# Causal mixers that project x before its root is known, with the root multiplied in behind the product

## The reference

```python
def first_block(x, norm_mix, w_in, w_pool, pool_scale, attn_gain, w_out, norm_ffn, ...):
    for l in range(DEPTH):
        h = rmsnorm(x, norm_mix[l])
        x = x + hybrid_mixer(h, w_in[l], w_pool[l], pool_scale[l], attn_gain[l], w_out[l])
        h = rmsnorm(x, norm_ffn[l])
        ...

def hybrid_mixer(h, w_in, w_pool, pool_scale, attn_gain, w_out):
    proj = h @ w_in
    u = proj[..., :D_POOL]
    q, k, v = jnp.split(proj[..., D_POOL:], 3, axis=-1)
    y_a = pool_mixer(u, w_pool, pool_scale)
    o = dilated_attention(to_heads(q), to_heads(k), to_heads(v))
    y_b = rmsnorm(o..., attn_gain)
    return jnp.concatenate([y_a, y_b], axis=-1) @ w_out
```

## Time and profile before

| | us |
|---|---|
| median of 3 runs | 2465.37 (2464.77 to 2465.46) |
| the profiled execution, its own time | 2464.63 |
| its span, from the first to the last instruction | 2462.4 |
| TensorE busy | 2427.3 (99%) |
| DVE busy | 2077.8 (84%) |
| ACT busy | 1576.1 (64%) |
| GpSimd busy | 172.1 (7%) |

### The profile page before, as it was taken

The page is one execution under the profiler, slowest core; times in us unless marked ns, Lnnn a source line. Parts: engine busy times, 40 slices in busy tenths (PEclk is TensorE's granted clock), DMA queues, the critical chain, the costliest instruction groups (busy, mean ns, idle before and its releaser), DMA issues.

```text
span 2462.4 us, 44463 instructions
## 1 busy us (share of the span) xinstructions
PE 2427.3 (99%) x17074; PEld 2223.3 (90%) x17074; DVE 2077.8 (84%) x2848; ACT 1576.1 (64%) x2312; POOL 172.1 (7%) x244
## 2 busy tenths in 40 slices
PE   9999999999999999999999999999999999999999
PEld 9999998999999999899998899988899899988998
DVE  5788867999999999999999799786898898787665
ACT  5644565888888888888887544557544544567543
POOL 2111021000000000000000111011011011010000
PEclk9999999999999999999999999999999999999999
DMA  7698554999999999999999688443688587432542
GB/s 297 230 364 312 201 180 174 395 361 378 364 384 365 381 371 396 396 396 398 396 385 376 220 320 308 162 146 129 240 314 304 215 319 291 155 129 81 219 181 76
DMA packets 136640, 696.22 MB, mean 283 GB/s; under 512 B 16528, under 2 KB 16656, under 8 KB 87728
## 3 DMA queue, kind: packets, MB, share of 16 engines
q1 hardware_dynamic: 109872, 598.79, 64.6%
q0 software_dynamic: 23424, 88.16, 9.4%
q10 hardware_dynamic: 3136, 6.43, 0.7%
HBM read 683.29 MB, written 13.24 MB: 283 GB/s over the span
## 4 chain that ended last, share of the span: by engine, by line
PE 86%; DVE 8%; ACT 4%; issue 2%; POOL 0%; DVEq 0%; ACTq 0%; POOLq 0%
PE ps L2451 16%; PE ps L2047 15%; PE ps L2048 15%; PE ps L2049 15%; PE ps L2617 10%; PE ps L2453 8%; DVE w_parts L1733 2%; DVE a_parts L1741 1%; ACT w_parts L1140 1%; DVE w_parts L1354 1%; PE ps L2072 1%; PE ps L2583 1%; PE ps L2076 1%; ACT w_parts L824 1%; DVE xT L1376 0%
## 5 line engine op out<-in xcount | busy, mean ns | idle before, releaser
L2451 PE MATMUL ps<-a_parts,w_parts 128*128 128x512 f32 x1760 | 618.8, 394 | 1.4 <-DVE a_parts L1319 1.0
L1733 DVE TENSOR_TENSOR w_parts<-ring,w_parts 128x1024 fp32r<-128x1024 f32 x448 | 548.3, 1224 | 42.3 <-ACT w_parts L1140 36.8
L2047 PE MATMUL ps<-w_parts 128*112 128x256 f32 x1792 | 517.0, 289 | 0.0
L2048 PE MATMUL ps<-w_parts 128*112 128x256 f32 x1792 | 500.1, 279 | 0.0
L2049 PE MATMUL ps<-w_parts 128*112 128x256 f32 x1792 | 500.0, 279 | 0.0
L2453 PE MATMUL ps<-a_parts,w_parts 128*128 128x256 f32 x1760 | 493.5, 280 | 0.0
L1140 ACT ACTIVATE w_parts<-ring 128x1024 fp32r<-128x1024 f32 x448 | 471.7, 1053 | 0.0
L2451 PEld LDWEIGHTS ps<-a_parts,w_parts 128*128 128x128 f32 x1760 | 329.9, 187 | 74.7 <-issue 3.5
L2453 PEld LDWEIGHTS ps<-a_parts,w_parts 128*128 128x128 f32 x1760 | 333.0, 189 | 0.0
L2048 PEld LDWEIGHTS ps<-w_parts 128*112 128x112 f32 x1792 | 313.3, 175 | 11.6
L2047 PEld LDWEIGHTS ps<-w_parts 128*112 128x112 f32 x1792 | 313.6, 175 | 10.9 <-issue 0.2
(11 more groups left out here) (286 smaller groups left out, 4379.2 us busy)
## 6 DMA issues: line engine op xcount, KB each, us to landing
ring<-wstream SPq DMA_DIRECT2D x378, 1024.0 KB, 7.3
ring<-wstream SPq DMA_DIRECT2D x378, 512.0 KB, 5.9
proj<-astream POOLq DMA_DIRECT2D x144, 512.0 KB, 5.8
slot_rows<-branch POOLq DMA_DIRECT2D x7, 448.0 KB, 7.3
slot_out<-slot_rows POOLq DMA_DIRECT2D x1, 3136.0 KB, 15.1
sq<-slot_rows ACTq DMA_DIRECT2D x49, 64.0 KB, 5.4
slot_out<-pT ACTq DMA_DIRECT2D x49, 64.0 KB, 5.4
vtok<-crow POOLq DMA_DIRECT2D x3, 512.0 KB, 4.3
```

The costliest lines, as they stand in the source:

```text
L1733: nc.vector.tensor_tensor(up_lo[:, n % 2, at], ring[:, s, at], up_hi[:, n % 2, at], ALU.subtract)\
L2047: mm(o, stationary[0], moving[0], start=start, stop=False, skip_group_check=True)
L2048: mm(o, stationary[0], moving[1], start=False, stop=False, skip_group_check=True)
L2451: mm(ps[:, bank, :], hi, a_parts[:, :, k, :], start=k == 0, stop=k == KB - 1, skip_group_check=True)
```

## The change

- In norms 0 and 2 (`RAW`) `hT` is no longer made. ACT writes `a_hi` as x times norm weight, beside each square; DVE makes the rest of the same product by one scalar_tensor_tensor with x and `a_hi` (`raw_rest`). In norm 2 these rests stand between the residual adds, two blocks behind.
- The head of tile 0 in norm 0 is split in thirds of 1024 between these, where it was in halves.
- TensorE starts the product first and makes the five sums just before block 7 of tile 0. The six fillers of these two norms are gone, and `WARM` goes from 24 to 30.
- ACT makes the root behind tile 1's high parts, into a row of its own (`root_row`).
- The units that are not values are copied by DVE (`scaled_unit`), which multiplies the root row and the constant scale in. They take their places among DVE's other work in the mixer, and the rests of tiles 2 to 4 are queued as halves between them. Units 0 to 3 go to banks 4, 5, 7 and 0.
- For the values the root is wanted by token: TensorE turns the root row by two fp32 matmuls of one column each into bank 7, ACT copies it, and ACT's copies of units 12 to 15 take it as their scale and wait for the twelve scaled units.

The diff, cut:

```diff
-WARM = 24
+WARM = 30
...
             if m < 2:
-                return n if n < 4 else 4 + n % 2
+                return (4, 5, 7, 0)[n] if n < 4 else 4 + n % 2
...
# ACT, norm(n)
                 for k in range(KB):
...
+                    if n in RAW:
+                        nc.scalar.activation(a_hi[:, k, :], xT[:, k, :], ACT.Identity,
+                                             scale=V("norm_mix", (n // 2) * KB + k)).then_inc(ah_ready, 1)
+                        if n == 0 and k in (1, 3, 5):
+                            head(0, k // 2)
                     nc.scalar.activation(sq[:, k, :], xT[:, k, :], ACT.Square,
...
-                if n == 0:
-                    head(n, 0)
+                if n in RAW:
+                    opened()
+                    hi_tile(HEADS[n], 1)
                 act.wait_ge(ss_ready, norm_at(n) + 1)
-                inverse_root(norm_s[:, 1, :], norm_s[:, 0, :], SS[:, 0:T],
+                inverse_root(root_row[:, :] if n in RAW else norm_s[:, 1, :], norm_s[:, 0, :], SS[:, 0:T],
...
# ACT, in_copies: values
+                            act.wait_ge(in_copied, UNITS_BEFORE[m] + IN1_F * FB)
+                            act.wait_ge(by_token, m + 1)
+                            nc.scalar.activation(vtok[:, tt, a:b], ps[:, bank, 0:b - a], ACT.Identity,
+                                                 scale=root_of[:, tt:tt + 1]).then_inc(in_copied, 1)
...
# ACT, mixer1
                 in_copies(m, 6, 8)
+                act.wait_ge(token_roots, m + 1)
+                nc.scalar.activation(root_of[:, :], ps[:, 7, 0:TT], ACT.Copy).then_inc(by_token, 1)
                 copy_turned(u)
...
# DVE
+                if n == 0:
+                    for k in range(KB):
+                        raw_rest(n, k)
+                        if k in (1, 3, 5):
+                            head(0, k // 2)
+                elif n == 2:
+                    head(2, 1)
...
+            def raw_rest(n, k):
+                dve.wait_ge(ah_ready, KB * SPLIT_INPUTS.index(f"n{n}") + k + 1)
+                if n:
+                    dve.wait_ge(x_ready, KB * (n - 1) + k + 1)
+                nc.vector.scalar_tensor_tensor(a_lo[:, k, :], xT[:, k, :], V("norm_mix", (n // 2) * KB + k),
+                                               a_hi[:, k, :], ALU.mult, ALU.subtract).then_inc(as_ready, 1)
...
# DVE, residual(r, gate=None, early=None, raw=None)
                 for k in range(KB):
+                    if raw and k >= 2:
+                        raw_rest(raw, k - 2)
...
+                for k in (KB - 2, KB - 1) if raw else ():
+                    raw_rest(raw, k)
...
# DVE, mixer1
-                lo_tiles(stage, [2])
+                def lo_part(i, h):
+                    lo(stage, i, *tile_half(stage, i, h), 2 * (SPLITS[stage] + i) + h, h == 1)
+
+                def scaled_unit(n):
+                    wait_unit(dve, m, n)
+                    if 4 <= n < 8:
+                        dst, scale = upad[:, n - 4, 16:16 + T], 1.0
+                    else:
+                        dst, scale = proj[:, QKV_DST[n], :], HD ** -0.5 if n in (0, 1, 8, 9) else 1.0
+                    nc.vector.scalar_tensor_tensor(dst, ps[:, unit_bank(m, n), 0:T], scale, root_row[:, :],
+                                                   ALU.mult, ALU.mult).then_inc(in_copied, 1)
+
+                dve.wait_ge(norm_root, norm_at(2 * m) + 1)
+                for n in range(3):
+                    scaled_unit(n)
+                lo_part(2, 0)
+                scaled_unit(3)
+                lo_part(2, 1)
+                scaled_unit(4)
                 dve.wait_ge(consts_loaded, 16 * 3)
                 masked(u, masks[0])
+                scaled_unit(5)
                 divided(u)
                 masked(u + 1, masks[1])
-                lo_tiles(stage, [3])
+                scaled_unit(6)
+                lo_part(3, 0)
+                scaled_unit(7)
+                lo_part(3, 1)
                 divided(u + 1)
-                lo_tiles(stage, [4, 5])
+                scaled_unit(8)
+                lo_part(4, 0)
+                scaled_unit(9)
+                lo_part(4, 1)
+                scaled_unit(10)
+                scaled_unit(11)
+                lo_tiles(stage, [5])
                 masked(u + 2, masks[0])
...
-            residual(1)
+            residual(1, raw=2)
...
# TensorE
                 for k in range(KB):
+                    if n in RAW and k == KB - 1:
+                        norm(n)
                     wait_head(n, k)
...
                     scores(u, 0, 4, 8)
+                    pe.wait_ge(norm_root, norm_at(2 * m) + 1)
+                    for tt in range(TT):
+                        ins = mm(ps[:, 7, tt:tt + 1], root_row[:, tt * P:(tt + 1) * P], C("ident")[:, 0:1],
+                                 start=True, stop=True)
+                    ins.then_inc(token_roots, 1)
```

More of the change, by code:

```diff
@@ L504, in head_part, with heads_before, h_before @@
                 return slice(half * D, (half + 1) * D)
-            cut = UP if n else TILE // 2
-            return slice(half * cut, cut + half * (TILE - cut))
+            if n == 0:
+                return slice(half * D, (half + 1) * D)
+            return slice(half * UP, UP + half * (TILE - UP))
+        def heads_before(n):
+            return 2 * HEAD_AT[n] + (n > 0)
+        RAW = (0, 2)
+        def h_before(n):
+            return KB * (n // 2)
         def norm_at(n):
@@ L512, in head_half @@
         def head_half(n, k):
-            if HEADS[n] not in FFN_STAGE and n:
+            if n == 0:
+                return {0: 0, D // COLS: 1, UP // COLS: 2}.get(k)
+            if HEADS[n] not in FFN_STAGE:
                 return {0: 0, UP // COLS: 1}.get(k)
@@ L779, in norm @@
                         .then_inc(both_roots, 1)
[L780 to L785, removed]
+                if n in HEADS and n not in RAW:
+                    opened()
+                if n == 1:
+                    split_input("n1", hT, h_ready, h_before(1))
                 elif n >= 5:
@@ L851, in in_copies @@
                         a, b = sum(cols[:v]), sum(cols[:v + 1])
-                        nc.scalar.activation(vtok[:, tt, a:b], ps[:, bank, 0:b - a], ACT.Copy)\
-                            .then_inc(in_copied, 1)
[L854 to L862, removed]
+                        if m < 2:
+                            act.wait_ge(in_copied, UNITS_BEFORE[m] + IN1_F * FB)
[3 more added lines that the diff above has]
+                        else:
+                            nc.scalar.activation(vtok[:, tt, a:b], ps[:, bank, 0:b - a], ACT.Copy)\
+                                .then_inc(in_copied, 1)
+                    elif m >= 2:
+                        nc.scalar.activation(proj[:, F_ORDER[at], :], ps[:, bank, 0:T], ACT.Copy,
+                                             scale=HD ** -0.5 if 13 <= F_ORDER[at] < 17 else 1.0)\
+                            .then_inc(in_copied, 1)
                     if last:
@@ L1277, in head @@
                 r, q = STARTS[HEADS[n]] % NS, SPLITS[HEADS[n]] % 2
-                dve.wait_ge(head_hi, 2 * HEAD_AT[n] + half + 1)
+                dve.wait_ge(head_hi, heads_before(n) + half + 1)
                 nc.vector.tensor_tensor(w_lo[:, q, at], ring[:, r, at], w_hi[:, q, at], ALU.subtract)\
@@ L1299, in norm @@
                                             w_hi[:, q, 0:D], ALU.subtract).then_inc(second_lo, 1)
-                if n == 0:
-                    head(0, 0)
-                dve.wait_ge(norm_root, norm_at(n) + 1)
+                if n not in RAW:
+                    dve.wait_ge(norm_root, norm_at(n) + 1)
                 def scaled(k):
@@ L1363, in lo_tiles, with residual @@
                         lo(stage, i, *tile_half(stage, i, h), 2 * (SPLITS[stage] + i) + h, h == 1)
-            def residual(r, gate=None, early=None):
+            def residual(r, gate=None, early=None, raw=None):
                 for k in range(KB):
+                    if raw and k >= 2:
+                        raw_rest(raw, k - 2)
                     if early and k == 6:
@@ L2073, in norm @@
                 ins.then_inc(ss_ready, 1)
-                if n in HEADS:
+                if n in HEADS and n not in RAW:
                     for _ in range(6):
-                        mm(ps[:, 7, 0:T], ones[:, :], xT[:, 0, :] if n == 0 else C("cos"), start=True, stop=True)
+                        mm(ps[:, 7, 0:T], ones[:, :], C("cos"), start=True, stop=True)
             def final_sum():
@@ L2088, in wait_head @@
                 if half is not None:
-                    pe.wait_ge(head_lo, 2 * HEAD_AT[n] + half + 1)
+                    pe.wait_ge(head_lo, heads_before(n) + half + 1)
                 wait_input(f"n{n}", k)
             def wait_h(n, k):
-                pe.wait_ge(h_ready, KB * n + k + 1)
+                pe.wait_ge(h_ready, h_before(n) + k + 1)
             def inproj(m, n):
@@ L2104, in inproj @@
                         at = k * COLS + b * P
```

(4 more changed lines are left out.)

23 lines of the change are left out of this document (15 added, 8 removed).

## The result

The changed kernel takes 2484.66 us (median of four runs, 2481.24 to 2485.80) against 2465.24: a ratio of 1.0077, 95% interval 1.0065 to 1.0088. It is slower, as I said, but by 19.4 us where I had forecast 6, and outside my range. The profiled execution is the fastest of the four, 2481.24, with a span of 2479.5 (17.1 more than before).

A forecast was written before the change was run, and what follows sets the result against it. TensorE, with 86% of the chain, was taken as the bound. Terms 0.1 - 1.1 + 0.9 + 6.6 = +6.5 on 2464.63 gave 2471.1, 2471.9 for the median; forecast 2471.5 us, range 2465.5 to 2475.

The forecast's parts named there:

- Heads: First weight tile of each mixer: mixer 0 +0.1 us (-0.4 to +0.8), mixer 1 a gain of 1.1 (0.6 to 1.5).
- Hold: DVE instructions with two SBUF tensors and GpSimd's exclude each other, first asker first; GpSimd's first window add 3.3 us, formerly 2.74.
- Root turns: Two fp32 matmuls per mixer putting the root by token into PSUM: 0.45 us per mixer, +0.9 together (0.4 to 1.2).
- Scalings: 24 unit copies moved from ACT to DVE at 0.48 us each: no TensorE wait, up to 1 us if one slips.
- list of signs: Trace signs to check; waits for DVE's scalings anywhere, or no TensorE wait for GpSimd, would make the prediction wrong.
- Window stall: Ahead of each mixer's pooling product, TensorE waits 3.3 us for GpSimd's last window step: +6.6 for both, the main term.
- Mixers together: Sum of heads, root turns and window stalls over both mixers: +6.5 us.
- rival 3: TensorE's clock falls to half rate for some 3 us in both stalls: +3.2, 2474.7 us; chance 0.10.

The follow-up runs named there:

- e3: The changed kernel with tile 3's two low-part operations (rests) on VectorE moved ahead of the scalings of units 6 and 7, in both mixers: 2476.87 us, ratio 1.0048.
- e7: The changed kernel with its two new tensors allocated last and tile 3's low parts ahead of the scaling of unit 6: 2465.06 us against 2464.71, ratio 1.0002.
- e1: The changed kernel with its two new tensors allocated last, so hid and the constants keep their old addresses: 2472.38 us, ratio 1.0029.
- e11: The changed kernel as it is, run again for a second profile and more times: median 2483.53 us, ratio 1.0072.
- e2: The kernel before with one unused tensor of 1056 bytes a partition where the change allocates its two: 2475.97 us, ratio 1.0044.
- e4: The kernel before with an unused tensor of 32 bytes a partition ahead of hid_hi: 2476.59 us, ratio 1.0045.
- e6: The kernel before with 64 unused bytes ahead of hid_hi, moving everything behind; total time not in the text, 51 slow FFN chunks of 100.
- e5: The kernel before with the 32 unused bytes behind hid_lo, so hid stays and small tensors and constants move; total time not in the text.
- e9: The kernel before with 32 unused bytes behind ones, so only cst, vec and wr move: 1.1 us above the 2468.3 expected.
- e10: The kernel before with the tensor order allocated last and 32 unused bytes ahead of cst, so ranks to ones move: 0.5 us above the 2464.7 expected.

## Why the prediction was right or wrong

- **Heads.** Mixer 0: first weight matmul forecast at 11.4, was 11.24; unit 3 at 23.05, was 22.88. Mixer 1: from the mark in the first FFN's last chunk to unit 3's first matmul the kernel before takes 17.02 (289.43 to 306.45), the changed one 15.38 (293.83 to 309.21). So this head gained 1.6, where I had 1.1 and at most 1.5. The wait of 1.4 for the last third was in my working without a name: five blocks from 292.4 end at 297.8, and I had the sixth at 299.65. Read against the mark it came 0.3 sooner, and unit 3 0.4 sooner.
- **Hold.** Right: mixer 0's pair adds took 1.40 to 1.57 each (0.70 alone), the first add 3.34 (3.3 forecast), the last step came behind tile 5's halves. e3 turns it round by order alone. The contention that the Trainium skill names (GPSIMD Engine Reference, the table at its head) is borne out by these times; that who asks first goes first is from these rows.
- **Root turns.** Forecast 0.45 each; in e7 the four matmul records of one (two fp32 matmuls) start at 29.57 and the next matmul at 30.04: 0.47.
- **Scalings.** 0.42 each instead of 0.48, and one wait of 0.41 for them at unit 3. The sum had it, but my list of signs counted any such wait against me: the two didn't agree.
- **Window stall.** 3.3 each forecast, 2.89 recorded. Taking it away brings 2.1 in mixer 0 (77.01 to 74.91) and 2.2 in mixer 1: in each, 0.24 of it stays and a new wait of 0.17 for a scaling appears, and the remaining 0.3 I didn't trace.
- **Mixers together.** Forecast +6.5 to the profiled execution; in it, +5.2. By stretches, mixer 0 and mixer 1: the head -0.4 and -1.6; from unit 3 to the pooling product +3.3 and +3.5, which is the stall and the root turn; from there to the late mark +0.2 each, cause open. With the clock's falls, which I had as rival 3 at 1.6 each and a chance of 0.10, +8.2 (e1: 3.13 + 1.50 and 2.03 + 1.59). The price came out right (1.50 and 1.59), in part by luck: the rows that I took it from give a granted clock of 1.00 in both stretches and so don't show a fall. The chance was far too low: my longest known wait was 1.5, and I took that nothing was shown as a reason for a small chance. The statement of the Trainium skill that I set beside it (TensorE: Matmul & The Clock Gate, Part 1), that idle time takes the array back to 1.2 GHz, agrees with the traces of e1 (granted clock 0.54) and e11 (0.53), and not with the changed kernel's first (1.00).
- **What failed.** The sum lacks a term. My count prices instructions and waits, and holds every matmul outside the mixers at its old time: it puts the two new tensors at nothing and gives no reason, though they by their place in the list of allocations move hid and cst. That term is 10.7 us by e2 and 12.3 by e1, and it put the result outside the range. e1, with only that undone, is at 2472.38, 0.9 from my 2471.5; so close is luck, since the mixers came out 1.3 under my count and the clock's falls, which it left out, 3.1 over.

Summed up for the median run: 5.2 for the mixers, 3.1 for the clock, 11 for the placement: 19.3 of 19.4. A sum this close is closer than its terms are known: the placement is 10.7 to 12.3, and the start of before alone varies by 1.0.

## What to carry to other kernels

Put a new SBUF tensor at the end of the allocations, and time a change against a kernel before that has the same addresses: 32 unused bytes cost this kernel 0.45%. Where two engines exclude each other, look at who asks first by tenths of a microsecond, and move one independent operation before giving up the change. And work that leaves the front of a stage must go into time in which the bounding engine waits anyway: the same products, with the sums kept ahead of the tile's arrival, turned no gain into 0.1%.

## What the runs showed of the hardware that I had not expected

- The issue rhythm of back-to-back matmuls has two patterns here (347 and 353.5 ns for a pair of 512 and 256 columns). The stream stays in one for hundreds of microseconds (e4, and before) or changes between them from chunk to chunk (e6). Which it does depends on the SBUF address of another tensor that TensorE reads in between. Why, and whether hid's place within 64 bytes is the rule (32 over a multiple of 64: quick in e5, e9, e10, and no slower in e6; 0 over: slow in e2 and e4), is open; for cst it isn't, since 64 bytes cost as much as 32.
- A TensorE wait of 2.89 us was followed by half clock in two traces and by full clock in a third of the same instructions, and the changed kernel's two sets of four executions spread over 4.6 and 4.1 us. The kernel before spreads over 3.1 in 33 executions on one chip, and over 4.3 in 19 on another, where all but one lie within 3.1.
- The kernel before starts its first weight matmul up to 1.0 us later from one execution to the next, and from there to the late mark of mixer 0 repeats within 0.04. In the latest two (e4, e10) TensorE's sums follow its fillers at 9.39 and 9.33, in the earliest at 8.34.
